# A hybrid decoder layer: residual rows turned raw for the router, one pair sooner, and twelve token tiles choosing experts inside the mixer

## The reference, cut to what matters

```python
h = h + hybrid_mixer(rms_norm(h, norm1_g), ...)       # ... merged @ w_out
xn = rms_norm(h, norm2_g)
g_prob = softmax(xn @ rg_w + rg_b); g_val, g_idx = top_k(g_prob, 1)
e_logits = (xn @ re_w + re_b).reshape(tokens, 4, 8)   # the 8 experts of the best group
e_val, e_idx = top_k(e_logits of group g_idx, 2)
weights = softmax(e_val) * g_val
# tokens sorted by expert, padded to blocks; each block: silu(x@w1)*(x@w3) @ w2, scaled, added to h
```

## Time and profile before

| | us |
|---|---|
| median of 3 runs | 2444.71 |
| lowest, highest | 2442.81, 2447.09 |
| profiled execution, its own time | 2440.6 |
| its span in the profile | 2438.8 |
| TensorE busy in the span | 2257.3 (93%) |
| VectorE, ScalarE, GpSimd busy | 1659.0, 1164.3, 792.5 |

### The profile page before, as it was taken

How to read it: one execution, slowest core, us unless ns; L and a number is a source line. 1 busy time by engine, 2 the same in 40 slices (tenths; PEclk the granted TensorE clock), 3 DMA queues, 4 the chain that set the end, 5 groups by cost and what they waited for, 6 DMA issues and landing times. The chain is left out here.

```text
span 2438.8 us, 34741 instructions
## 1 busy us (share of the span) xinstructions
PE 2257.3 (93%) x10908; PEld 1757.8 (72%) x10909; DVE 1659.0 (68%) x2642; ACT 1164.3 (48%) x1690; POOL 792.5 (32%) x600
## 2 busy tenths in 40 slices
PE   6999989799999999999997998599999999999991
PEld 4777868678888888878886776477667676677771
DVE  7698777678887757888674655765556555566665
ACT  4533333244444334444431332476557665677663
POOL 3831101322321001120000000467556655558771
PEclk9999999999999999999999999699999999999995
DMA  7964846626564295665358442599778888789987
GB/s 206 375 225 181 310 144 223 181 92 195 172 204 146 96 370 172 221 204 172 117 180 315 159 155 107 214 313 340 265 257 287 300 285 292 259 300 375 322 288 293
DMA packets 248453, 567.80 MB, mean 233 GB/s; under 512 B 35550, under 2 KB 136158, under 8 KB 230176
## 3 DMA queue, kind: packets, MB, share of 16 engines
q1 hardware_dynamic: 231856, 508.77, 58.4%
q0 software_dynamic: 16496, 57.74, 9.4%
HBM read 445.85 MB, written 120.59 MB: 232 GB/s over the span
## 5 line engine op out<-in xcount | busy, mean ns | idle before, releaser
L1932 PE MATMUL mrgps<-x_blocks,w_hi 128*128 128x512 f32 x1568 | 488.8, 393 | 17.2 <-DMA x_blocks<-xn_feature_major 9.7
L1932 PEld LDWEIGHTS mrgps<-x_blocks,w_hi 128*128 128x128 f32 x1568 | 293.3, 189 | 82.4 <-DMA x_blocks<-xn_feature_major 10.0
L2561 POOL TENSOR_TENSOR w_lo<-w_raw,w_hi 128x1024 fp32r<-128x1024 f32 x128 | 344.1, 2828 | 0.0
L2725 PE MATMUL exps<-w_hi,x_room 128*128 128x512 f32 x1024 | 330.9, 399 | 3.0 <-DVEq L2896 3.0
L1730 ACT ACTIVATE w_hi<-w_raw 128x512 fp32r<-128x512 f32 x268 | 159.6, 627 | 336.3 <-DMA w_raw<-in_merge_gate_w_dram 159.7
L1932 PE MATMUL mrgps<-x_blocks,w_lo 128*128 128x512 f32 x784 | 306.4, 391 | 0.0
L2556 DVE TENSOR_TENSOR w_lo<-w_raw,w_hi 128x2048 fp32r<-128x2048 f32 x127 | 284.5, 2301 | 0.0
L2023 DVE TENSOR_TENSOR w_lo<-w_raw,w_hi 128x512 fp32r<-128x512 f32 x268 | 189.5, 722 | 98.8 <-ACT w_hi L1730 98.1
L2546 ACT ACTIVATE w_hi<-w_raw 128x2048 fp32r<-128x2048 f32 x128 | 239.2, 1920 | 9.1 <-DMA w_raw<-in_expert_w_dram 9.1
L2725 PEld LDWEIGHTS exps<-w_hi,x_room 128*128 128x128 f32 x1024 | 193.2, 189 | 62.0 <-issue 16.9
L2725 PE MATMUL exps<-w_lo,x_room 128*128 128x512 f32 x512 | 202.4, 395 | 0.0
(11 more groups left out here) (476 smaller groups left out, 4516.9 us busy)
## 6 DMA issues: line engine op xcount, KB each, us to landing
w_raw<-in_expert_w_dram SPq DMA_DIRECT2D x192, 1024.0 KB, 8.7
w_raw<-in_merge_gate_w_dram SPq DMA_DIRECT2D x32, 1024.0 KB, 5.8
ys_lo<-branches SPq DMA_DIRECT2D x64, 512.0 KB, 4.8
win_hi<-w_in_parts SPq DMA_DIRECT2D x42, 512.0 KB, 3.9
win_lo<-w_in_parts SPq DMA_DIRECT2D x42, 512.0 KB, 5.6
w_out_blocks<-branch_rows SPq DMA_DIRECT2D x64, 256.0 KB, 5.6
x_blocks<-w_out_blocks SPq DMA_DIRECT2D x6, 2048.0 KB, 16.7
w_raw<-in_x_dram SPq DMA_DIRECT2D x16, 512.0 KB, 8.7
```

The source lines that it names most:

```text
L1932: last = pe.matmul(bank[bk][:], ring[w][:, f % RING, j], x_block(b, x, j), start=(start and j + s == 0), stop=(j == HALF - 1 and s == 2), ...
L2561: eng.tensor_tensor(self.lo2[:, f], self.raw2[:, f], self.hi2[:, f].bitcast(F32), ALU.subtract).then_inc(self.split2, 1)
L2725: last = pe.matmul(bank[:], x[:, k], weights[:, 2 * w + k // 4, cols], start=(k + i == 0), stop=(k == KD - 1 and i == 2))
```

## The change

- `turn` transposes the raw residual rows (after `rows_set`) and no longer the scaled ones; channels are taken as c*8+k, and norm2_g is multiplied into the router weights by GpSimd. The logits are scaled afterwards: `logit` is now (product x inverse root) + bias.
- The router of pair r-1, not r-2, runs in step r, so it starts in step 1; only pair 7 is left behind the last product, written out with a second transposed room in two free banks.
- On VectorE the 12 small instructions go to the head of the step, the two scalings behind "22". On ScalarE both squares of the pair before stand around `first_copy`.
- `load_router` goes from SyncE to the GpSimd queue, right after the last merge; the weights are loaded as 128 rows of 128 B and of 1024 B, and copied to their layout by the multiplication.
- In step 7 VectorE chooses the experts of the first twelve tiles (`early`); `route` does the last four (`late`). Tiles are counted in the order in which they are made.
- `hot`, `below` and `ones` are fp32r, so each rank product is one pass. GpSimd adds `hot` for twelve tiles.
- The end of `merge_branches` no longer waits for the last stores; `route` does, on GpSimd and VectorE, before `hot` is written. The last scalings stand behind the last `norms` and between the last logits.

```diff
             def turn(r, t):
-                pe.wait_ge(n_full, 2 * r + t + 1)
+                rows_set.reached(pe, (NA + r, row_done(NA + r, t)))
...
-                        last = pe.transpose(..., xn(r)[:, t, (4 * h + kk) * P:(4 * h + kk + 1) * P], ident)
+                        last = pe.transpose(..., xr(r)[:, t].rearrange("p (c k) -> p k c", k=KD)[:, 4 * h + kk], ident)
...
             for q in range(NA + 1, NQ):
                 product(q, 0)
-                if r > 1:
-                    turn(r - 2, 0)
+                turn(r - 1, 0)
                 product(q, 1)
                 product(q, 2)
-                if r > 1:
-                    rout(r - 2, 0)
-                    turn(r - 2, 1)
+                rout(r - 1, 0)
+                turn(r - 1, 1)
...
-            for r in range(NQ - 2 - NA, NQ - NA):
-                turn(r, 0)
-                rout(r, 0)
-                turn(r, 1)
-                back(r, 0)
-                rout(r, 1)
-                back(r, 1)
+            q, r = NQ - 1, NQ - 1 - NA
+            turn(r, 0)
+            rout(r, 0, range(0, 4))
+            rows_set.reached(pe, (q, "21"))
...
+                    last = pe.transpose(last_banks[h][:, kk * P:(kk + 1) * P], xr(r)[:, 1]..., ident)
+            rout(r, 0, range(4, 8))
+            pe.wait_ge(last_copy, 2)
...
+                if kk == 4:
+                    back(r, 0)
+                last = pe.matmul(rbank[1][0:R, 0:P], rw[:, kk], xnT_last[:, kk], ...)
+            back(r, 1)
 # VectorE
+                if final:
+                    dve.wait_ge(pool_set, 3)
+                    early.group(dve, s)
+                    early.members(dve, s)
+                norms(r - 1)
+                second(q)
                 part_low(q, "s3")
                 part_low(q, "s4")
-                second(q)
                 part_low(q, "22")
+                if final:
+                    early.first(dve, s)
+                    early.second(dve, s)
+                else:
+                    scaled(r - 1, 0)
+                    scaled(r - 1, 1)
                 third(q)
                 residual(q, "11")
+                if final:
+                    early.second_hot(dve, s)
                 corner(q, "22")
                 residual(q, "22")
...
+            norms(r)
+            logit(r, 0)
+            scaled(r, 0)
+            logit(r, 1)
+            scaled(r, 1)
 # GpSimd
+            def load_router(q):
+                for c in corners["gate"]:
+                    pool.wait_ge(acc_out[c], 16 * KD)
+                pool.dma_start(g2, io["norm2_g"][0:1].partition_broadcast(P)).then_inc(g2_in, 16)
+                for dst, src in ((rg_raw, ...), (re_raw, ...), (rb[:, 0:G], ...), (rb[:, G:R], ...), (g2c, ...)):
+                    pool.dma_start(dst, src, allow_slow_non_contiguous=True).then_inc(rpar_in, 16)
 # route, VectorE
+            late.group(dve, s)
+            late.members(dve, s)
+            late.first(dve, s)
+            late.second(dve, s)
+            late.second_hot(dve, s)
+            for stored in last_out:
+                dve.wait_ge(stored, 16 * TT // 2)
+            TTc(hot[:, TT - LATE:], oh[0][:, TT - LATE:], oh[1][:, TT - LATE:], ALU.add).then_inc(hot_ready, 1)
```

More of the change, by code:

```diff
@@ L1346, in merge_branches @@
         ring = [sb(f"w_{n}", [P, RING, HALF, P], F32R) for n in ("hi", "lo")]
-        wb = [sb(f"wb_{n}", [P, 2, QW], F32R) for n in ("hi", "lo")]
-        acc = sb("merged", [P, 2, 2, TC])
+        kept_sums = sb("merged", [P, 2, TC])
+        acc = (kept_sums[:], choice.rearrange("p (t c) -> p t c", t=2))
         first_part, u2z = sb("first_part", [P, TC]), sb("u2_z", [P, 2, TC])
@@ L1424, in chunk @@
         def chunk(m, t):
-            return PAIRS[m][t] * TC
+            return CHUNKS[m][t] * TC
         def item_raw(i):
@@ L1662, in _ @@
                 store_xn(NQ - 1, t)
-            for t in range(2):
-                sp.wait_ge(h_out[t], 16 * TT // 2)
-                sp.wait_ge(n_out[t], 16 * TT // 2)
+            sp.wait_ge(h_out[0], 16 * TT // 2)
+            sp.wait_ge(n_out[0], 16 * TT // 2)
         @block.gpsimd
@@ L2237, in _ @@
                 residual(q, "12")
-                if q + 1 < NQ:
+                logit(r - 1, 0)
+                logit(r - 1, 1)
+                if final:
+                    scaled(r - 1, 1)
+                else:
                     part_low(q + 1, "s1")
@@ L2242, in _, with route @@
             r = NQ - 1 - NA
-            norms(r, slice(0, 1))
-            norms(r, slice(1, 2))
-            for i in (r - 1, r):
-                logit(i, 0)
-                logit(i, 1)
-def route(nc, dram, logits, table, dest, ends, wt):
+            dve.wait_ge(t_full, 4 * r + 3)
+            dve.tensor_copy(xnT_last[:, 0:4].rearrange("p k t -> p (k t)"), last_banks[0][:]).then_inc(last_copy, 1)
+            norms(r)
[3 more added lines that the diff above has]
+            scaled(r, 1)
+def route(nc, dram, logits, choice, scales, last_out, table, dest, ends, wt):
     with ExitStack() as ctx:
@@ L2339, in _ @@
             sp.wait_ge(w_row_set, 1)
-            for m in range(TT // 4):
-                rows = dram["xn"][1 + 4 * P * m:1 + 4 * P * (m + 1), D:D + E]
+            for m, c in enumerate(CHUNKS[0] + CHUNKS[1]):
+                rows = dram["xn"][1 + 4 * P * c:1 + 4 * P * (c + 1), D:D + E]
                 sp.dma_start(rows.rearrange("(p q) e -> p q e", q=4), w_row[:, 4 * m:4 * m + 4]).then_inc(w_row_out, 16)
@@ L2561, in write_low2, with run_experts @@
             eng.tensor_tensor(self.lo2[:, f], self.raw2[:, f], self.hi2[:, f].bitcast(F32), ALU.subtract).then_inc(self.split2, 1)
-def run_experts(nc, io, dram, table, dest, scales, ends, wt, out):
+def run_experts(nc, io, dram, choice, table, dest, scales, ends, wt, out):
     HC = 256
@@ L2583, in run_experts @@
         hT = sb("hT_half", [P, FE, HB])
+        c_ssq, c_msq, c_rst, c_rh, c_rt = (sb(f"c_st{i}", [P, TT]) for i in range(5))
         up_row = sb("up_rows", [HB, 2, HC])
```

353 lines of the change are left out of this document (202 added, 151 removed).

## The result

| | before | after |
|---|---|---|
| median of the runs beside the first result | 2445.90 us (4 runs, 2442.81 to 2447.53) | 2403.98 us (4 runs, 2402.28 to 2404.53) |
| the same again, more runs | 2442.30 us (19 runs, 2439.22 to 2447.36) | 2404.57 us (5 runs, 2401.37 to 2409.47) |
| profiled execution, its time and span | 2440.6, 2438.8 | 2404.0, 2402.3 |

Ratio 0.9829, 95% interval [0.9812, 0.9846]; again 0.9843 [0.9828, 0.9857]. The kernel is faster by 1.6 to 1.7%, some 38 to 42 us. 2408 was forecast, 4 too many; 36.7 us were to go from the profiled execution, and 36.5 went.

The account below looks back on a forecast made before the run. Bound: TensorE, busy 93% of the span, so time in which it is not fed counts. -0.6 + 5.6 + 11.3 + 12.5 + 7.9 = 36.7 us off the median 2444.7 gives 2408.0; 8 in 10: 2401 to 2418.

Parts of the forecast that it names:

- from the profiled execution to the median: Last step of the sum: the median stood 4.1 us above the profiled execution, so 2444.7 - 36.7 = 2408.0.
- Part 1: Projection steps 3 to 7: without TensorE's stalls a step takes 25.8 us, not 28.06; 2.25 saved in each, 11.3 us.
- Part 2: Steps 1 and 2, router start: step 2 starts 0.6 us later, then takes 25.8 instead of 31.4, 5.6 saved.
- the zero row's 5.05: Landing of a small GpSimd transfer beside expert-weight loads, 5.05 us; used to put the router weights' landing at 1307.
- norm2_g's 16.4: Landing of norm2_g before, 16.4 us behind SyncE's blocks; with that it would come at 1312.4, 4 us late, absorbed by cover.
- GpSimd's loads are late: Rival: router loads on GpSimd late by queueing, `rout` of step 1 waits up to 4 us, 2409 to 2412; 6%.
- GpSimd is held by VectorE: Rival: each of GpSimd's six issues waits for a VectorE instruction, `rout` waits 1.5 to 9 us, 2410 to 2417; 4%.
- Part 3: Tail, last product to `route`: 9.4 us instead of 21.95, ended by the last scaling; 12.5 us saved.
- Part 4: Start of `route` to the scan: 8.5 us instead of 16.4, 7.9 saved, of which the fp32r product 0.5.
- Margins behind the scan: Between scan and gather: margins of 4.5 us for `w_row` and 2.4 for its store ahead of the gather; priced at nothing.
- GpSimd becomes the bound of route: Rival: zero row or last stores land 5 us later, the gather moves by 2.6 and more, 2411 to 2415; 12%.
- Early choice: Step 7: VectorE chooses experts of twelve tiles at no cost on TensorE, margin 3.7 us, any excess paid in full.

Follow-up runs that it names:

- second trace of before: The kernel before, unchanged, run and profiled again: median 2442.09 us (10 runs), ratio to before 0.9998; its profiled execution took 2445.5.
- the version with what was found: Changed kernel with five router loads ahead of norm2_g, all `hot` additions on VectorE, `late.group` sooner, last scaling partly on ScalarE: 2404.80 us, 0.9838 against before.

## Why the prediction was right, and where it was not

- **The step that failed: from the profiled execution to the median.** "The median stood 4.1 above that execution, and the same shift gives" 2408. That shift was three runs against one, not a property of the kernel. 19 runs put before at 2442.3, 1.7 above its profiled execution, and less the 36.7 that is 2405.6; measured 2404.0 to 2404.6. The sum of 36.7 came true against this one trace (36.5), with the luck that the ledger shows.
- **Part 1, the chain in a step.** Right in mechanism and size: 25.63 against 25.8. In the step from 1429.42 the first product takes 2.73 (forecast 2.72), the turn 0.80 (0.84), the second product 2.84 (2.88), and the rest 19.26 (19.35); no term is off by a tenth. The order alone takes 1.53 of the 2.44 away without a raw row. What part 1 did not say is that the residual must be early for the turn: with the old order the step is 30.8, longer than the 28.06 of before.
- **Part 2, the router's start.** Right sum (5.3 against 5.0; 6.6 by the second trace of before), wrong reason for the cover. The landing was taken from the zero row's 5.05; these took 12.6 to 13.7 (below). The prediction had the weights at 1307 for a need at 1312.9; they were there at 1309.3 for 1310.4. Its own other row, norm2_g's 16.4, was the nearer one. The rival "GpSimd's loads are late" gave the wait up to 4 us; it came in one run, 3.30, and cost 6.1, more than the wait. Over half of that wait is the rival "GpSimd is held by VectorE", in the multiplication of the weights and not in the issues, where the prediction looked.
- **Part 3, the tail.** 9.68 against 9.4; the last scaling ends the block, as it said. It is read from the profile; no run takes a part of the tail back.
- **Part 4, route.** The wrong term of the sum. 8.5 to the scan became 9.93, and "behind the scan nothing changes" became 1.1 more. 0.8 of the first and 1.8 of the second (of which before paid 0.65 in its one `tensor_scalar`, 0.84 instead of 0.19) are VectorE standing beside GpSimd; the other 0.6 of the first were not taken apart. The prediction had this only the wrong way round, as VectorE holding up GpSimd's loads; the six issues took 0.55 to 0.58 us each, so in the issues that did not come. fp32r gave 0.3 and not 0.5.
- **Margins behind the scan.** The gather waited for nothing but its index, in the changed kernel and with `w_row` begun 2.6 us later; the rival "GpSimd becomes the bound of route" did not come as a late store, but as a shared port.
- **Early choice.** Free on TensorE, as forecast; worth 4.6 by the traces, 5.9 by the medians.

## What to carry to other kernels

When a consumer is moved ahead (here the turn of a row, one pair sooner), cost the old order with the new consumer too: the two halves of this change are worth 2.4 us a step together, the order alone 1.5, and rows turned raw and sooner without the order make a step 2.7 us longer than it was (30.76 against 28.06). For a transfer's landing take the row of the same moment, not of the same size, and issue small loads as early as their room is free. Read a saving from the trace against the trace, and turn it into a median only with many runs of the kernel before. Price a wide GpSimd operation next to a chain of tiny VectorE ones: here one cost VectorE 0.8 of its 1.0 us, and three in a row 1.8 of their 3.4; beside an operation that reads PSUM it cost nothing.

## What the runs showed of the hardware

Five small router loads (128 KB for the experts' weights, 2 to 16 KB for the others) took 12.6 to 13.7 us to land from GpSimd, and 13.9 to 14.4 from SyncE's queue 10 us later. The windows around their issue, in the changed kernel:

```profile
1278.00:1292.00 14.00, 10.77 (x44) 8.49 (x43) 4.48 (x7) 0.63 (x1) 0.34 (x3) 0.93 1.03 393
1292.00:1306.00 14.00, 14.00 (x64) 11.66 (x63) 3.36 (x6) 4.75 (x9) 3.26 (x6) 0.95 1.01 419
```

All 16 engines are busy throughout (share 1.01 to 1.03, about 400 GB/s). Issued at 1275 to 1277, beside engines as full (1.02 from 1275 to 1290), the same loads took 6.1 to 9.1, and 6.1 to 8.9 in the version with what was found; so fullness alone does not give the time. A rival stands untested: where they were slow, the 512 KB of norm2_g stood right ahead of them in the same queue (landing 11.8 us after its issue from GpSimd, 15.7 from SyncE), and where they were quick it stood behind them. No run moves it alone. The Trainium skill, page "DMA: Bandwidth & Descriptors", section "Issuing engines are not separate DMA queues", says that transfers of all issuing engines run on the same 16 and interleave. By that, the trace agrees as far as it goes: the same loads were about as slow from either engine.

A wait costs TensorE more than itself. Waits of 3.37, 6.43, 9.33 and 3.30 us came with 1.8, 1.6, 1.7 and 2.8 us more of busy time in the step than the 25.64 without a wait, at a mean granted clock of 0.94, 0.90, 0.86 and 0.89 (the levels are 1.2 and 2.4 GHz; in the steps without a wait the clock is 1.00). So the extra did not grow with the wait. In the last case the loss is nearly twice the wait that the chain shows.

The hold between VectorE and GpSimd goes both ways. GpSimd's two multiplications of the router weights took 0.82 us in six traces, 1.44 to 1.68 in the four where VectorE's low parts (0.69 us each) had begun ahead of them, and 2.58 in the one where VectorE's scalings (1.24 us each) had.
